# A two-block model on one core: the router's logits in two banks, one mask load and three small loads moved, and the last expert's down matrix loaded and multiplied by column halves

## The reference

```python
# end of the first block
h = h + expert_choice_ffn(rmsnorm(h, norm_ffn_w), router_w, w_gate, w_up, w_down)

def expert_choice_ffn(xn, ...):
    probs = softmax(xn @ router_w)                 # 16 experts
    gate, idx = top_k(probs.T, 32)                 # each expert takes 32 tokens
    xg = xn[idx]
    h = silu(xg @ w_gate) * (xg @ w_up)            # [32, 2048], each expert 8 MB + 8 MB
    y = (h @ w_down) * gate                        # [32, 1024], 8 MB
    return zeros.at[idx].add(y)

x = rmsnorm(h, norm_final_w)                       # end of the first block
# start of the second block
h = rmsnorm(x, norm_mix_2)
proj = h @ w_in_2      # q, k, v of both mixers; ki (32 columns), gdown (16), wi (8), ogate
```

## Time and profile before

| what | value |
|---|---|
| median of three runs | 1424.22 us |
| the profiled execution's own time | 1424.23 us |
| its span, first to last instruction | 1422.4 us |
| mean granted TensorE clock | 0.899 |
| TensorE busy | 1092.7 us, 77% of the span |
| VectorE, ScalarE, GpSimd busy | 26%, 22%, 22% |
| shares of the chain that ended last | DMA 57%, PE 40%, DVE 2%, ACT 1% |
| HBM read | 475.88 MB |

### The profile page before, as it was taken

How to read it: one execution, slowest core, us unless ns; L and a number is a source line. 1 busy time by engine, 2 the same in 40 slices (tenths; PEclk the granted TensorE clock), 3 DMA queues, 4 the chain that set the end, 5 groups by cost and what they waited for, 6 DMA issues and landing times.

```text
span 1422.4 us, 19705 instructions
## 1 busy us (share of the span) xinstructions
PE 1092.7 (77%) x8358; PEld 629.3 (44%) x8358; DVE 369.9 (26%) x755; ACT 305.9 (22%) x457; POOL 307.7 (22%) x216
## 2 busy tenths in 40 slices
PE   7999997556756656666575665666678999999998
PEld 7998732111211211211031121121125988999997
DVE  6586530000100001000010010000104857553333
ACT  5753210000000000000000000000004636454443
POOL 6796000000000000000000000000003785386661
PEclk9999999888877888888888888888899999999999
DMA  9513999999999999999999999999999832575540
GB/s 288 186 34 121 389 425 428 427 428 427 428 428 428 429 428 428 429 428 429 428 428 429 429 428 428 428 429 427 428 428 330 220 119 92 178 249 178 178 149 30
DMA packets 95288, 478.06 MB, mean 336 GB/s; under 512 B 11098, under 2 KB 64217, under 8 KB 70393
## 3 DMA queue, kind: packets, MB, share of 16 engines
q1 hardware_dynamic: 94528, 476.30, 83.2%
q10 hardware_dynamic: 697, 0.84, 0.2%
HBM read 475.88 MB, written 1.25 MB: 335 GB/s over the span
## 4 chain that ended last, share of the span: by engine, by line
DMA 57%; PE 40%; DVE 2%; ACT 1%; issue 0%; SPq 0%; DVEq 0%; ACTq 0%
PE bank L1321 21%; DMA ring<-in_expert_w_down 20%; DMA ring<-in_expert_w_up 18%; DMA ring<-in_expert_w_gate 18%; PE bank L1024 4%; PE bank L2113 4%; PE bank L1046 2%; PE bank L410 1%; PE bank L427 1%; DMA ring<-in_w_in 1%; PE bank L1061 1%; PE bank L423 1%; PE bank L1515 0%; PE bank L1496 0%; PE bank L442 0%
## 5 line engine op out<-in xcount | busy, mean ns | idle before, releaser
L1024 PE MATMUL bank<-ring,work 128*32 128x512 f32 x2000 | 306.2, 745 | 201.6 <-DMA ring<-in_expert_w_up 124.4
L1024 PEld LDWEIGHTS bank<-ring,work 128*32 128x32 f32 x2000 | 60.5, 123 | 435.6 <-DMA ring<-in_expert_w_up 200.4
L1295 POOL TENSOR_TENSOR slot_r<-ring,slot_r 128x512 fp32r<-128x512 f32 (+1 forms) x123 | 226.8, 1873 | 102.5 <-ACT slot_r L1267 102.4
L1304 POOL TENSOR_TENSOR slot_r<-ring,slot_r 128x512 fp32r<-128x512 f32 x16 | 21.9, 1392 | 956.3 <-ACT slot_r L1273 956.3
L1046 PE MATMUL bank<-ring,work 128*32 128x512 f32 x1024 | 155.3, 741 | 85.8 <-DMA ring<-in_expert_w_down 81.0
L1321 PE MATMUL bank<-slot_r 128*128 128x256 f32 (+2 forms) x1080 | 160.5, 288 | 3.8 <-DVE tokm_r L2475 1.8
L1321 PEld LDWEIGHTS bank<-slot_r 128*128 128x128 f32 (+1 forms) x1080 | 145.2, 192 | 8.0 <-issue 5.3
L1098 DVE TENSOR_TENSOR work<-work,bank 128x512 f32<-128x512 f32 x16 | 11.0, 688 | 491.2 <-PE bank L1024 491.2
L1321 PE MATMUL bank<-work_r,slot_r 128*128 128x256 f32 x704 | 129.1, 283 | 0.2 <-DVE chan_r L1836 0.2
L1108 DVE SCALAR_TENSOR_TENSOR hres<-bank,work,hres 128x512 f32<-128x512 f32 x64 | 48.1, 751 | 276.0 <-PE bank L1061 272.8
L1267 ACT ACTIVATE slot_r<-ring 128x2048 fp32r<-128x2048 f32 x62 | 116.7, 1904 | 3.2 <-DMA ring<-in_w_in 3.2
(11 more groups left out here) (419 smaller groups left out, 1046.6 us busy)
## 6 DMA issues: line engine op xcount, KB each, us to landing
ring<-in_expert_w_down SPq DMA_DIRECT2D x64, 2048.0 KB, 35.7
ring<-in_expert_w_gate SPq DMA_DIRECT2D x63, 2048.0 KB, 36.0
ring<-in_expert_w_up SPq DMA_DIRECT2D x62, 2048.0 KB, 35.8
ring<-in_w_in SPq DMA_DIRECT2D x23, 1024.0 KB, 8.2
ring<-in_w_ffn_gate SPq DMA_DIRECT2D x11, 1024.0 KB, 5.7
ring<-in_w_ffn_up SPq DMA_DIRECT2D x11, 1024.0 KB, 5.4
ring<-in_w_ffn_down SPq DMA_DIRECT2D x11, 1024.0 KB, 4.9
ring<-in_w_out SPq DMA_DIRECT2D x8, 1024.0 KB, 5.0
```

Source lines behind the costliest of these rows:

```text
L1024: ins = pe.matmul(bank[b][32 * j:32 * j + 32, :], xg[:, 2 * s + kk, a * CAP:(a + 1) * CAP], w_[kk][:, j * W5:(j + 1) * W5], start=(s == 0 ...
L1295: ins = eng.tensor_tensor(ring_r[s][:, a:a + step], ring[:, s, a:a + step], ring_r[s][:, a + UNIT:a + UNIT + step].bitcast(F32), ALU.subtract)
L1304: ins = eng.tensor_tensor(ring_r[s][:, at:at + q], ring[:, s, at:at + q], ring_r[s][:, at + UNIT:at + UNIT + q].bitcast(F32), ALU.subtract)
```

## The change

Six edits:

1. The router's logits of the two token tiles go to banks 2 and 5 instead of side by side into bank 2, and each tile signals and is reduced by itself.
2. The half of piece 1 that goes to `masks` is issued right behind piece 3.
3. Of the last expert, the four down pieces are (half of the output columns, half of the rows): each comes in two DMAs of 1 MB with rows of 2 KB. TensorE (`last_down`) makes the first 512 output columns from pieces 20 and 21, scatters, and transposes half of `hres`; then the same for the other half from pieces 22 and 23. ScalarE and VectorE make `xh2` and `xl2` for channel blocks 0 to 3 between the halves.
4. The three loads of `kgw` are issued by ScalarE on its own queue, ahead of its work on the last pair's first expert, and `kgw` is split by ScalarE and VectorE inside the last expert.
5. `xh2`, `xl2` move from slot 6 to slot 7, the attention's `bias` from 7 to 6, `kgw` to the work tile, one square's scratch to `chan`.
6. SyncE's loop stops one pair earlier; the last pair's 24 loads are written out.

```diff
-                    ins = pe.matmul(bank[2][:, t * E:(t + 1) * E], chan[:, k, t * P:(t + 1) * P], rw[:, k, :],
+                    ins = pe.matmul(bank[LOGITS[t]][:, 0:E], chan[:, k, t * P:(t + 1) * P], rw[:, k, :],
...
-            ins.then_inc(S.route_out, 1)
+                ins.then_inc(S.route_out, 1)
@@ def last_down(pe, i): new, in place of the down and scatter loops of the last expert
+            for dh in range(2):
+                for part in range(2):
+                    w_ = expert_piece(pe, i, PAIR * SPE - 4 + 2 * dh + part)
+                    for c in range(2):
+                        for q in range(4):
+                            at = q * P + 32 * (2 * part + c)
+                            ins = pe.matmul(bank[YB[dh]][32 * q:32 * q + 32, :], hT[:, at:at + 32], w_[c][:, q * W5:(q + 1) * W5],
+                                            start=(part + c == 0), stop=(part + c == 2))
+                    ins.then_inc(S.slot_used, 1)
+                    if part == 0:
+                        keep_array_busy(pe, 6, XB if dh == 0 else YB[0])
+                if dh == 0:
+                    pe.wait_ge(S.selT_ready, E)
+                pe.wait_ge(S.y_ready, 2 * E - 1 + dh)
+                for t in range(TT):
+                    pe.matmul(bank[LAST_SB[t][dh]][:, :], selT[:, t * P:(t + 1) * P],
+                              yo[:, dh * W5:(dh + 1) * W5], start=True, stop=True).then_inc(S.scat_out, 1)
+                x2_transposes(pe, (2 * dh, 2 * dh + 1))
@@ def expert_pair_act(act, i, last=False):
                 act.wait_ge(S.slot_used, SPE * (PAIR * i + a) + 4)
+                if last and a == 0:
+                    small_weights(act)
                 act.activation(sg, bank[GB][:, :], ACT.Silu).then_inc(S.silu_ready, 1)
...
                 if last and a == PAIR - 1:
                     act.activation(warm, eps, ACT.Sqrt)
-                act.wait_ge(S.slot_used, SPE * (PAIR * i + a) + SPE)
+                    act.wait_ge(S.rel_in, 80)
+                    act.activation(kgw_hi, kgw_w, ACT.Copy).then_inc(S.act_chain, 1)
+                act.wait_ge(S.slot_used, SPE * (PAIR * i + a) + SPE - (2 if last and a == PAIR - 1 else 0))
+        def small_weights(act):
+            w3 = io["w_in_2"].rearrange("o (k p) c -> (o p) k c", p=P)
+            for at, c, w in ((0, KI, IDX_DIM), (IDX_DIM, GD, GATE_RANK), (IDX_DIM + GATE_RANK, WI, IDX_HEADS)):
+                act.dma_start(kgw_w[:, :, at:at + w], w3[:, :, c:c + w]).then_inc(S.rel_in, 16)
@@ def expert_pair_dve(dve, i, last=False):
                 if last and a == PAIR - 1:
-                    dve.wait_ge(S.slot_used, SPE * E)
-                    dve.tensor_copy(yo[:, W5:2 * W5], bank[YB[1]][:, :]).then_inc(S.y_ready, 1)
+                    dve.wait_ge(S.act_chain, 4)
+                    dve.tensor_tensor(kgw_lo, kgw_w, kgw_hi.bitcast(F32), ALU.subtract).then_inc(S.chan_ready, 1)
                 for n, (t, dh) in enumerate(scatter_order(last and a == PAIR - 1)):
+                    if last and a == PAIR - 1 and n == 2:
+                        lower_parts(dve, "x2", "norm_mix_2", X2B, xh2, xl2, range(DK // 2))
+                        dve.wait_ge(S.slot_used, SPE * E)
+                        dve.tensor_copy(yo[:, W5:2 * W5], bank[YB[1]][:, :]).then_inc(S.y_ready, 1)
@@ def load_slot(sp, i, n, masks_only=False):
+            elif isinstance(i, int) and i == E // PAIR - 1 and n >= PAIR * SPE - 4:
+                slot, half, part = (n - 1) % RING, s // 2, s % 2
+                at = (E - 1) * per + part * 2 * rows
+                for j in range(2):
+                    piece = flat[at + j * rows:at + (j + 1) * rows, half * W5:(half + 1) * W5].rearrange("(p k) c -> p k c", p=P)
+                    sp.dma_start(ring[:, slot, j * UNIT:(j + 1) * UNIT].rearrange("p (k c) -> p k c", k=4), piece).then_inc(slot_in[slot], 16)
@@ def experts_sync(sp):
                 load_slot(sp, 0, n)
+                if n == 3:
+                    load_slot(sp, 0, MASK_PIECE, True)
@@ def second_sync(sp):
                 load_unit(sp, SECOND_FIRST + n, w3[:, :, SECOND_COLS[n]:SECOND_COLS[n] + UC], DK)
-                if n == 0:
-                    for at, c, w in ((0, KI, IDX_DIM), (IDX_DIM, GD, GATE_RANK), (IDX_DIM + GATE_RANK, WI, IDX_HEADS)):
-                        sp.dma_start(kgw_w[:, :, at:at + w], w3[:, :, c:c + w]).then_inc(slot_in[7], 16)
             sp.wait_ge(S.slot_used, total)
-            sp.wait_ge(slot_in[7], landed(7, "second", 3))
@@ def second_act(act):
+            upper_parts(act, "x2", "norm_mix_2", X2B, xh2, range(DK // 2))
             for i in range(4):
                 split_high_part(act, SECOND_FIRST, i)
-            upper_parts(act, "x2", "norm_mix_2", X2B, xh2)
-            act.wait_ge(slot_in[7], landed(7, "second", 3))
-            act.activation(kgw_hi, kgw_w, ACT.Copy).then_inc(S.act_chain, 1)
+            upper_parts(act, "x2", "norm_mix_2", X2B, xh2, range(DK // 2, DK))
             split_high(act, SECOND_FIRST + 1)
@@ def second_dve(dve, link):
-            lower_parts(dve, "x2", "norm_mix_2", X2B, xh2, xl2)
+            lower_parts(dve, "x2", "norm_mix_2", X2B, xh2, xl2, range(DK // 2, DK))
...
-            dve.wait_ge(S.act_chain, 4)
-            dve.tensor_tensor(kgw_lo, kgw_w, kgw_hi.bitcast(F32), ALU.subtract).then_inc(S.chan_ready, 1)
```

More of the change, by code:

```diff
@@ L779, in build @@
         sems("spread_ready sel_ready idx_cols_ready")
-        ROUTED = {"logits": 1, "probT": 2, "places": 3, "idx_col": 4}
+        ROUTED = {"first": 1, "logits": 2, "probT": 3, "places": 4, "idx_col": 5}
+        LOGITS = (2, 5)
         rw = wab[:, :, :]
@@ L986, in expert_piece @@
             s = FIRST_PLACE[n] if first and n in FIRST_PLACE else (n - 1) % RING
-            pe.wait_ge(slot_in[s], 48 * i + landed(s, "experts", 1 if first and n in FIRST_PLACE else (n - 1) // RING + 1 - (s < 2)))
+            halves = isinstance(i, int) and i == E // PAIR - 1 and n >= PAIR * SPE - 4
+            pe.wait_ge(slot_in[s], 48 * i + 16 * halves + landed(s, "experts", 1 if first and n in FIRST_PLACE else (n - 1) // RING + 1 - (s < 2)))
             return ring[:, s, 0:SLOT // 2], ring[:, s, SLOT // 2:]
@@ L1040, in expert_pair @@
                 pe.wait_ge(S.hTm_ready, PAIR * i + a + 1)
+                if last and a == PAIR - 1:
+                    last_down(pe, i)
+                    return
                 for s in range(4):
@@ L1152, in experts_sync @@
                 load_slot(sp, 0, n)
-            with sp.Fori(1, E // PAIR) as i:
+            with sp.Fori(1, E // PAIR - 1) as i:
                 for n in range(PAIR * SPE):
@@ L1156, in experts_sync @@
                     load_slot(sp, i, n)
+            for n in range(PAIR * SPE):
+                sp.wait_ge(S.slot_used, PAIR * SPE * (E // PAIR - 1) + n - RING + 1)
+                load_slot(sp, E // PAIR - 1, n)
         def mix1_wout(sp, units):
@@ L1635, in build, with x2_transposes @@
         X2B = (2, 7, 3, 4)
+        def x2_transposes(pe, pieces):
+            for i in pieces:
+                if i % 2 == 0:
+                    pe.wait_ge(S.scat_added, 4 * E - 2 + i)
+                for k in (2 * i, 2 * i + 1):
+                    for t in range(TT):
+                        ins = pe.transpose(bank[X2B[i]][:, (k % 2) * T + t * P:(k % 2) * T + (t + 1) * P],
+                                           hres[:, t, k * P:(k + 1) * P], ident)
+                ins.then_inc(S.xT_out, 1)
         squares2 = work0[:, 9 * W5:11 * W5]
@@ L1822, in second_pool, with upper_parts @@
             biases(range(12, 16))
-        def upper_parts(act, name, weight, banks, high):
-            for k in range(DK):
+        def upper_parts(act, name, weight, banks, high, ks=range(DK)):
+            for k in ks:
                 if k % 2 == 0:
```

82 lines of the change are left out of this document (37 added, 45 removed).

## The result

The changed kernel takes 1428.14 us (median of 10 runs, 1425.77 to 1430.08), the kernel before 1424.11 us beside it (10 runs, 1423.07 to 1425.7): ratio 1.0026, 95% interval 1.0018 to 1.0034. That is 4.0 us slower, clear of the noise, where the forecast was +0.05 us. That the range reaches this far is luck: its top was drawn for a rival, a clock that falls in the last expert, and that did not happen.

What follows compares the result with a forecast made beforehand. DMA was taken to bound the expert stage until the last down piece lands, then steps waiting on each other up to `rows(1)`. Terms +1.4 + 2.0 - 3.35 = +0.05 took 1424.23 to 1424.3 us; range 1420.9 to 1428.

Steps and rivals of the forecast that it cites:

- a clock that falls in the last expert: Rival: in the last expert, fewer fillers let TensorE's clock drop to 1.2 GHz, giving 1427.5 us; chance 0.11.
- Start of the full stretch: From 156 us the DMA engines run without pause; issuing the mask half later was claimed to move that start by 0.
- 2 KB rows: Last four down pieces: the shorter rows were claimed to delay TensorE's start on the last piece by +1.4 us.
- kgw in the full stretch: Last pair: kgw's three loads of small rows were claimed to add +2.0 us to the DMA engines' pause-free time.
- kgw late: Rival, last pair: kgw's small rows wait turns beside large rows, landing near 1103 (1452 us) or 1199 (1549 us); chance 0.06.
- the decision point: ScalarE's queue, last pair: below 35 small rows a us, kgw would land after ScalarE's first copy of `y` is due.
- TensorE free at T0, and T0 to rows(0): Tail: TensorE is just free when the last down piece lands; `rows(0)` starts +6.8 us behind that, before +8.87.
- The norm's factors: Before `rows(1)`: reciprocal out about +15.4 us after the last down piece lands, fitting with less than half a microsecond.
- the -3.35: From TensorE's start on the last down piece to `rows(1)`: +16.25 us where it was +19.60, so -3.35 us.
- What is won or lost by the start of `rows(1)` I carry to the end one for one: Behind `rows(1)` TensorE goes on nearly without a pause, so any shift of its start reaches the end in full.
- Small rows are free: Rival: 2 KB rows and kgw cost nothing in the pause-free DMA time, 1420.9 us; chance 0.20 together with the mask half counting.
- 2 KB rows go like 1 KB rows: Rival, last four down pieces: the new rows move as slowly as 1 KB rows, +3.1 us, 1427.4 us; chance 0.07.

Runs made afterwards that it cites:

- e6: The kernel before with only the mask half issued later and the router's logits split; 1423.33 us, ratio 0.9993.
- e2_nohalf: The changed kernel without the column halves (16 KB rows, four adds, 16 transposes again); 1427.54 us, ratio 1.0019.
- e1_fifo: The changed kernel with the three kgw loads on SyncE's queue inside the last pair; 1429.74 us, ratio 1.0035.
- e3_fifo_nohalf: The changed kernel without the column halves and with the kgw loads on SyncE's queue in the last pair; 1425.02 us, ratio 1.0006.
- e5_pool: The changed kernel with GpSimd held back from unit 1 and the repeat copy until VectorE has made its sums; 1427.06 us, ratio 1.0020.
- e12_order: The kernel before with mask and router edits and a reordered tail (kgw's upper products first, reciprocal earlier, GpSimd waiting), no load moved; 1424.45 us, ratio 1.0003.
- e8_idle_nohalf: The changed kernel without column halves, GpSimd held back until VectorE's sums, kgw gathered in DRAM at 121 us; 1425.15 us, ratio 1.0009.
- e9_fill: The changed kernel with ten useless matmuls between the kgw matmuls and the wait for the norm's factors; 1427.26 us, ratio 1.0026.
- e4: The kernel before with only the last four down pieces loaded in two DMAs each with 2 KB rows; 1425.88 us, ratio 1.0013.
- e11: The changed kernel measured and profiled again, unaltered; 1430.17 us, ratio 1.0042.

## Why the prediction missed

**Start of the full stretch: right, as far as the profiles tell.** Forecast 0. The early piece is issued at 153.81 in before and at a mean of 153.73 in the twelve profiles with the edit, 152.43 to 155.58, and e6's stretch is as long as before's (+0.03). The reason given fits: with the mask half gone from the batch, 142 to 154 moves less (268 GB/s for 351) and nothing comes sooner.

**2 KB rows: mechanism right, size too small.** The working had three rates, 408 (one microsecond of the earlier trace rows), 386 (the point between 1 KB and 16 KB rows, if a row has a fixed price) and 428. It took +1.4 between the first two. The runs have 387 GB/s and +2.1 to +2.2: a fixed price for a row fits, and the single microsecond should have had no weight. The Trainium skill (DMA: Bandwidth & Descriptors, Specifications) puts line rate at 512 B and more; 348, 387 and 428 GB/s at 1, 2 and 16 KB disagree.

**kgw in the full stretch: right.** +2.0 forecast, +2.2 and +2.4 measured. The two terms give +4.2 to +4.6 where +3.4 was written: 1 us of the miss.

**The rival "kgw late": its mechanism was there, and luck kept it from showing.** Beside 16 KB rows the small rows do pass one for one with SyncE's (288 beside 288), not by the partition, as I read the earlier trace rows (no run shows whether ScalarE's queue had rows waiting all the time there, nor in the earlier trace rows), and not as the Trainium skill has it (DMA: Bandwidth & Descriptors, Queues, rings and completion order: whole packets of typically 9 to 17 descriptors in turn). At 28.8 rows a us the 3072 rows would take 107 us; the decision point was 35. By 1020, where the forecast had all of them through, 911 were. So the chance of 0.06 rested on a misreading, and my "27 us at worst" was wrong. The 2 KB rows of the same change saved it: they quicken the turns to 152 a us, a coupling that I didn't see. The price if it comes late was wrong too: e2_nohalf, without them, lost 1.5 us in its profile and not 28. That the hold-up is short because ScalarE's queue is empty was wrong too: 36.26 us, longer than SyncE's 30.22; that it is covered was right (e1_fifo).

**TensorE free at T0, and T0 to rows(0): right.** Idle 0.78 us before the last piece, `rows(0)` at +6.41 for +6.8 forecast, no wait in front of the kgw matmuls, which end at 15.2 behind T0 (forecast 15.85).

**The norm's factors: the step that failed.** The prediction had GpSimd make `tokm` until +12.2 and the reciprocal out at about +15.4, and put its lateness in before down to L1848 standing ahead. In after `tokm` is ready at +13.4, the two-column step (L1900) at +17.1, the reciprocal at +18.4: 3.0 us late, where I had half a microsecond to spare and a bound of one. I added up durations that each engine has when alone, and took L1848's 3.20 us as what the split costs. 448 elements a partition in 3.20 us, beside GpSimd's 1024 in 2.41, stood in the earlier trace rows and should have been asked about. The split costs 0.61; the other 2.6 were standing still beside GpSimd. Taking it out of that place freed next to no VectorE time: in e3_fifo_nohalf the sum inherits just these 2.6 us, and in after, where VectorE comes to the sum 2.3 us earlier behind T0 than in e3 and GpSimd's next instructions come 1.0 later, the sum (L1897) loses 2.2 and the two-column step (L1900) 2.4, so more than before. The standing still is shown for L1900 by e5_pool and for the split by e12_order; for the sum by its 1.21 us in e8_idle_nohalf and e12_order against 3.42 to 3.82 wherever an instruction of GpSimd's is under way. What isn't shown is that the forecast's +16.25 can be had: no run started `rows(1)` before +18.21. The Trainium skill (SBUF — State Buffer, Who interferes with whom) states just this rule: a VectorE instruction with two SBUF inputs, beside one of GpSimd that reads SBUF, or in a mode that takes both ports, contends for a shared pair of ports, and the lock is exclusive. The trace agrees with the ends of each within 0.15 us. It spoke against the -3.35, and I didn't weigh it.

**"What is won or lost by the start of `rows(1)` I carry to the end one for one": failed too.** The 3.1 us of waiting are in one piece and right in front of `rows(1)`; the granted clock is 0.50 behind it (1.2 GHz), and `rows(1)` takes 1.3 us longer (e9_fill: 5.99). Before, 1.54 us of waiting did no such thing. The rival with a fallen clock looked for it in the last expert, where it stays at 1.00.

**The other rivals.** "Small rows are free" is refuted by e4 and e2, "2 KB rows go like 1 KB rows" by 387 GB/s where it needs 348.

Together: T0 1.1 later than forecast, the start of `rows(1)` 2.8 (-0.56 for -3.35), the clock 1.3: 5.2 over the forecast's +0.05, which is what the table has (+4.47 and +0.75). e11's profile has 5.4 by the same terms. The medians have 4.0 in the first ten runs and 5.8 in e11's five. The other 0.65 of the two spans lies before the stretch, in the part that also differs between the two profiles of after; how much the terms behind it vary from run to run isn't settled.

## What to carry to other kernels

Before you credit the removal of a wait, ask whether the awaited instruction is long by itself: compare its time per element with a like one, and look for another engine whose instruction ends when it does. If so, its neighbours can inherit the stall, and then the gain isn't there. Count small rows twice: by the DMA time that they add to a full stretch, and by the turns that they need beside large rows, from the packet counts of both queues in one window.

## What the runs showed of the hardware

- VectorE stands still beside GpSimd, by whole instructions: 0.17 became 2.58 us, 0.61 became 3.20, 1.21 became 3.42, and 1.22 became 5.96 to 8.00 where GpSimd's instructions follow each other closely. GpSimd's own 2.41 became 3.38. Instructions that read a bank (four of L1886, 1.66 us) took as long beside GpSimd as without it.
- Two queues with rows waiting took turns row by row: 288 of 0.13 KB and less beside 288 that are nearly all of 16 KB in 10 us, 610 beside 609 in 4 us once these were of 2 KB.
- An engine that issues loads of many small rows is held for a part of the time that they drain: ScalarE 36.26 us for 3072, of which 911 had gone by then; the last went near 1068.
- Rows of 2 KB move 387 GB/s over 12 us.
- A gap of 3.1 us on TensorE behind a busy stretch was followed by a granted clock of 0.50 and cost 1.1 to 1.5 us in three profiles; with ten matmuls in it and 0.93 us of waiting left, the clock stayed at 1.00. Two gaps of 1.1 us did either, and so did one of 1.4.
